# Stick-breaking heads: value products moved behind the next head's scores, result copies ahead of the sigmoids

## The chip, the cores and the metric

The program runs on one core of one Trainium2 chip. The metric is the device time of one launch in microseconds (us). Its engines are TensorE (PE in the profile; its weight loads are a row of their own, PEld), VectorE (DVE), ScalarE (ACT), GpSimd (POOL) and the queue that issues the weight transfers (SP). They run their own instruction streams in order and meet at semaphores.

## The reference

A small language model of two blocks on 512 tokens of width 1024, in fp32. The second block has four layers; layers 0 and 3 mix tokens by "stick-breaking" attention with 8 heads of width 128. Cut to that mixer:

```
for i in range(seq // 128):
    end = (i + 1) * 128
    z = einsum('bhqd,bhkd->bhqk', q[i-th 128 rows], k[:end])
    mask = key < query
    u = where(mask, softplus(z), 0.0)
    a = where(mask, exp(z - rev_cumsum(u)), 0.0)
    out_i = einsum('bhqk,bhkd->bhqd', a, v[:end])
```

The kernel computes the same weights as sigmoid(z) times a running product of sigmoid(-z) from the right. Each of these layers goes on with a memory attention of 4 small heads, an output projection and a gated feed-forward net. Layer 1 has differential attention, layer 2 a short convolution.

## The kernel before, in words

Large matrix products run in three passes on fp32 data split into a high and a low part (high x high, low x high, high x low; function `three`, lines 2625 to 2627, and lines 3369 to 3371 and 3383 to 3385). ACT copies a weight unit to its high part `whi` (line 869), DVE subtracts that from the raw unit and leaves the low part `wlo` (line 1563).

In a stick-breaking layer the input projection is cut in units `n` of 256 output columns, and each unit in four quarters. One quarter is 12 products of 512 columns (or 24 of 256) on PE. Before each quarter stands a slot: slot number `s = 4 * n + q`. Work on the heads is hung into the slots by tables written by hand. For head `h` (0 to 7):

- slot `KQK[h]`: ACT copies q and k of the head to `qk_hi`, DVE makes `qk_lo`.
- slot `KZ[h]`: PE makes the scores z in PSUM (lines 3299 and 2625 to 2627, called "scores" here). ACT takes two sigmoids of them in the same slot (`rest`, then `stick`). One slot later DVE does what I call the chain: a maximum with `upper` in two pieces (line 2379), four scans that form the running product (line 2383), two maskings (line 2388) and the product `stick * rest` (line 2390).
- slot `KTURN[h]`: PE transposes `stick`, 10 blocks of 128x128 (line 3283, "turn"), after the chain has ended. ACT copies the result to `sticks_t` and `sticks_hi`, DVE makes `sticks_lo` (line 2395).
- slot `KPV[h]`: PE multiplies the turned weights with the values (lines 2625 to 2627 on `sticks_hi`, `sticks_lo`, `v_hi`, `v_lo`, then line 3275 in plain fp32; "value product") into PSUM bank 3. It waits for `sticks_lo`, for `v_lo` of its pair of heads, and from the second head on until the result before it has left bank 3. `v_hi` and `v_lo` are made once for two heads, by the even one, two slots ahead of its value product: `at_slot(KPV, s, -2)`. DVE's subtraction for `v_lo` is line 2399, and stands last in its slot.
- the result: ACT copies bank 3 to the high part of `act2`, one slot after the value product (line 1438); DVE subtracts for the low part (`mix_low`, line 2315), two slots after.

Within one slot PE does the value product first, then the turn, then the scores, then the quarter. Slots of the next and the last head interleave: scores of head 1 are in slot 24, between the turn of head 0 (23) and the turn of head 1 (27). In a slot that begins a unit DVE also evicts the last half unit (line 2546, or 2543 for values) and makes `wlo`; it evicts the first half of a unit two slots later.

Of the kernel before, what the change touches and what calls it, by code (L numbers as in the profile page):

```python
# [26 lines left out]
ACT = mybir.ActivationFunctionType  # L27
# [15 lines left out]
NH2, DH2 = 8, 128  # L43
# [29 lines left out]
def wq(i):  # L73
    return P * (i + 1)
# [27 lines left out]
KZ = [20, 24, 28, 32, 36, 40, 47, 52]  # L102
KTURN = [23, 27, 31, 35, 39, 43, 51, 55]
KQK = [18, 22, 26, 30, 34, 38, 46, 50]
KPV = [25, 29, 33, 37, 41, 45, 53, 56]

DZ = [20, 28, 36, 48]

# [2 lines left out]
def at_slot(table, s, after=0):  # L111

    return [h for h, n in enumerate(table) if n is not None and n + after == s]
# [29 lines left out]
def build(nc, A, out, ext_dram):  # L143
    with ExitStack() as ctx:
        sems = {}

        def S(name):
            if name not in sems:
                sems[name] = ctx.enter_context(nc.semaphore(name))
            return sems[name]  # L150
# [3 lines left out]
        def at(name, offset, shape, dt=F32):  # L154
            return nc.alloc_sbuf_tensor_at(name, shape, dt, offset=offset)
# [12 lines left out]
        act2 = at("act2", A0, [P, KF, 2, T], F32R)  # L168
# [114 lines left out]
        def bank(b, w=BANK, off=0):  # L283
            return ps[:, b * BANK + off:b * BANK + off + w]
# [91 lines left out]
        mix_hi, mix_ready = S("mix_hi"), S("mix_ready")  # L376
# [21 lines left out]
        def g_in(l):  # L398
            return G_L0 + sum(evictions(m) + 25 for m in range(l))
# [4 lines left out]
        def evicted(n, half):  # L404

            return n + 1 if n < 2 else 2 + 2 * (n - 2) + half + 1
# [9 lines left out]
        def unit_of(p, stream):  # L416

            return 1 + 3 * p + stream if p >= 2 else (1 + 4 * p + stream if stream < 2 else 3)

        def values_taken(p, last):  # L420

            return evicted(unit_of(p, 2) + (p < 2 and last), 1 if p < 2 else last)
# [90 lines left out]
        def bc(ap2, n):  # L513

            m = ap2.shape[1]
            return ap2.rearrange("p (a m) -> p a m", a=1).broadcast_to([P, n, m])
# [342 lines left out]
        def _(act):  # L859
            a = nc.scalar  # L860
# [556 lines left out]
            def stick_slot(idx, s):  # L1417
                for h in at_slot(KQK, s):
                    n, l = NH2 * idx + h, 3 * idx
                    act.wait_ge(acc_free, g_in(l) + evicted(unit_of(h // 2, 1), h % 2))  # L1420
                    if n:
                        act.wait_ge(S("k_z"), n)
                    for m, b in enumerate((qp, kp)):
                        a.activation(qk_hi[:, m, :], b[h // 2 % 2][:, h % 2, :], ACT.Copy).then_inc(S("qk_hi"), 1)
                for h in at_slot(KPV, s, -2):
                    if h % 2 == 0:
                        n = NH2 * idx + h
                        act.wait_ge(acc_free, g_in(3 * idx) + values_taken(h // 2, 0))
                        if n:
                            act.wait_ge(S("k_o"), n)  # L1430
                        a.activation(v_hi[:, :, :], vp[h // 2 % 2][:, 0:2, :], ACT.Copy).then_inc(S("v_hi"), 1)
                for h in at_slot(KZ, s):
                    act.wait_ge(S("k_z"), NH2 * idx + h + 1)
                    a.activation(rest[:, 0:ZW], ps[:, 0:ZW], ACT.Sigmoid, scale=-1.0).then_inc(S("k_sigmoid"), 1)
                    a.activation(stick[:, :], ps[:, 0:ZW], ACT.Sigmoid).then_inc(S("k_sigmoid"), 1)
                for h in at_slot(KPV, s, 1):
                    act.wait_ge(S("k_o"), NH2 * idx + h + 1)
                    a.activation(act2[:, h, 0, :], bank(3), ACT.Copy).then_inc(mix_hi, 1)
                for h in at_slot(KTURN, s):
                    n = NH2 * idx + h  # L1440
                    act.wait_ge(S("k_tr"), n + 1)
                    if n:
                        act.wait_ge(S("k_o"), n)
                    a.activation(sticks_t[:, :], ps[:, WIDE:ZW], ACT.Copy).then_inc(S("k_at"), 1)
                    a.activation(sticks_hi[:, :], ps[:, 0:WIDE], ACT.Copy).then_inc(S("k_at"), 1)
# [35 lines left out]
            def slot_step(l, s):  # L1481
                memory_slot(l, s)
                if l == 1:
                    differential_slot(s)
                else:
                    stick_slot(l // 3, s)
# [56 lines left out]
        def _(dve):  # L1543
# [3 lines left out]
            def link(ins):  # L1547

                chain[0] += 1
                ins.then_inc(S("vec_chain"), 1)  # L1550
                dve.wait_ge(S("vec_chain"), chain[0])
# [761 lines left out]
            def mix_low(slot, src, n):  # L2313
                dve.wait_ge(mix_hi, n + 1)
                v.tensor_tensor(act2[:, slot, 1, :], src, act2[:, slot, 0, :].bitcast(F32), ALU.subtract).then_inc(mix_ready, 1)
# [50 lines left out]
            def stick_slot(idx, m0, s):  # L2366
                if s == KZ[0]:
                    link(v.memset(rest[:, ZW:ZW + 8], 1.0))
                for h in at_slot(KQK, s):
                    for m, b in enumerate((qp, kp)):  # L2370
                        dve.wait_ge(S("qk_hi"), 2 * (NH2 * idx + h) + m + 1)
                        v.tensor_tensor(qk_lo[:, m, :], b[h // 2 % 2][:, h % 2, :], qk_hi[:, m, :].bitcast(F32),
                                        ALU.subtract).then_inc(S("qk_lo"), 1)
                for h in at_slot(KZ, s, 1):
                    n = NH2 * idx + h
                    dve.wait_ge(S("k_sigmoid"), 2 * n + 1)
                    for b0, step in ((ZQ[0], 384), (ZQ[3] + 384, 256)):
                        d = bass.AP(tensor=rest[:, :].tensor, offset=b0, ap=[[ZW + 8, P], [step, 2], [1, P]])
                        v.tensor_tensor(d, d, bc(upper[:, :], 2), ALU.max).then_inc(S("k_step"), 1)
                    dve.wait_ge(S("k_step"), 9 * n + 2)  # L2380
                    for i in range(4):
                        r = rest[:, ZQ[i]:ZQ[i] + wq(i)][:, ::-1]
                        v.tensor_tensor_scan(out=r, data0=r, data1=ones[:, 0:1].broadcast_to([P, wq(i)]), initial=1.0,
                                             op0=ALU.mult, op1=ALU.mult).then_inc(S("k_step"), 1)
                    dve.wait_ge(S("k_sigmoid"), 2 * n + 2)
                    for b0, step in ((ZQ[0], 384), (ZQ[3] + 384, 256)):
                        d = bass.AP(tensor=stick[:, :].tensor, offset=b0, ap=[[ZW, P], [step, 2], [1, P]])
                        v.tensor_tensor(d, d, bc(mask[:, :], 2), ALU.mult).then_inc(S("k_step"), 1)
                    dve.wait_ge(S("k_step"), 9 * n + 8)
                    v.tensor_tensor(stick[:, :], stick[:, :], rest[:, 1:ZW + 1], ALU.mult).then_inc(S("k_step"), 1)  # L2390
                for h in at_slot(KPV, s, 2):
                    mix_low(h, bank(3), m0 + 2 + h)
                for h in at_slot(KTURN, s):
                    dve.wait_ge(S("k_at"), 2 * (NH2 * idx + h) + 2)
                    v.tensor_tensor(sticks_lo[:, :], ps[:, 0:WIDE], sticks_hi[:, :].bitcast(F32), ALU.subtract).then_inc(S("k_al"), 1)
                for h in at_slot(KPV, s, -2):
                    if h % 2 == 0:
                        dve.wait_ge(S("v_hi"), NH2 * idx + h // 2 + 1)
                        v.tensor_tensor(v_lo[:, :, :], vp[h // 2 % 2][:, 0:2, :], v_hi[:, :, :].bitcast(F32), ALU.subtract).then_inc(S("v_lo"), 1)
# [73 lines left out]
            def attention_slot(l, s):  # L2473
                if l == 1:
                    differential_slot(8 + 10 * l, s)
                else:
                    stick_slot(l // 3, 8 + 10 * l, s)
# [30 lines left out]
            for l in range(NL):  # L2508
# [3 lines left out]
                m0 = 8 + 10 * l  # L2512
# [107 lines left out]
        def _(pe):  # L2620
# [640 lines left out]
            def stick_slot(l, s):  # L3261
                base, m0 = NH2 * (l // 3), 8 + 10 * l
                for h in at_slot(KPV, s):
                    pe.wait_ge(S("k_at"), 2 * (base + h + 1))
# [225 lines left out]
```

## Time and profile before

| | |
|---|---|
| median of 3 runs | 2963.1 us (2962.44 to 2963.11) |
| the profiled execution: its own time | 2963.98 us |
| its span | 2962.3 us |
| PE busy | 2948.2 us (100% of the span) |
| PE weight loads busy | 2652.0 us (90%) |
| DVE busy | 2260.7 us (76%) |
| ACT busy | 1469.7 us (50%) |
| mean granted TensorE clock | 0.999 of full speed |

Busy times are sums over the profiled execution; the engines overlap. The own time is 1.7 us longer than the span, for what lies before the first and behind the last instruction. The two stick-breaking stages lie at about 689 to 835 us and 2427 to 2573 us of the span.

### The profile page before, as it was taken

The numbers are of one execution on the slowest core, as the hardware profiler recorded it, in microseconds if no ns is written. First come the engines' busy times: TensorE is split into PE (matmuls) and PEld (weight loads), VectorE is DVE, ScalarE is ACT, GpSimd is POOL, SyncE is SP. The second block draws the span as 40 slices with busy tenths as digits, with TensorE's granted clock in tenths as the row PEclk, the third lists the DMA queues.
The fourth block names the chain that finished last, engine by engine and source line by source line (L and its number), as shares of the span: only waits on it lengthen the run. The fifth ranks groups of instructions, "written<-read, shape, count | busy, mean of one in ns | idle before, by whom it ended". The sixth has DMA issues, their size and how long they took to land.

```text
span 2962.3 us, 47955 instructions
## 1 busy us (share of the span) xinstructions
PE 2948.2 (100%) x18733; PEld 2652.0 (90%) x18733; DVE 2260.7 (76%) x2788; ACT 1469.7 (50%) x2168; POOL 60.9 (2%) x148
## 2 busy tenths in 40 slices
PE   9999999999999999999999999999999999999999
PEld 8779999888889999878899998888999888889998
DVE  7979888567659887577598875658988568589884
ACT  4576555455345555444455543325555344355553
POOL 6100000000000000000000000000000000000000
PEclk9999999999999999999999999999999999999999
DMA  6232333341133333311333233223333222133332
GB/s 204 60 96 86 113 113 105 109 138 62 56 102 100 99 107 100 105 57 54 106 100 99 96 111 99 82 75 113 107 99 107 93 86 66 56 114 106 99 107 86
DMA packets 261720, 286.98 MB, mean 97 GB/s; under 512 B 12547, under 2 KB 233921, under 8 KB 261577
## 3 DMA queue, kind: packets, MB, share of 16 engines
q1 hardware_dynamic: 261320, 284.69, 30.1%
q8 instruction: 102, 1.67, 0.2%
q14 instruction: 42, 0.34, 0.0%
q10 hardware_dynamic: 256, 0.28, 0.0%
HBM read 280.73 MB, written 5.78 MB: 97 GB/s over the span
## 4 chain that ended last, share of the span: by engine, by line
PE 95%; DVE 3%; ACT 1%; issue 0%; DMA 0%; POOL 0%; ACTq 0%; POOLq 0%; SPq 0%; DVEq 0%
PE ps L2973 40%; PE ps L2625 14%; PE ps L2627 14%; PE ps L2626 14%; PE ps L3383 1%; PE ps L3385 1%; PE ps L3384 1%; PE ps L3283 1%; PE ps L3350 1%; PE ps L3369 1%; PE ps L3370 1%; PE ps L3371 1%; PE ps L3229 1%; PE ps L2876 0%; PE ps L3218 0%
## 5 line engine op out<-in xcount | busy, mean ns | idle before, releaser
L869 ACT ACTIVATE whi<-raw 128x2048 fp32r<-128x2048 f32 (+2 forms) x144 | 246.6, 1712 | 478.7 <-PE ps L2627 371.5
L1563 DVE TENSOR_TENSOR wlo<-raw,whi 128x2048 fp32r<-128x2048 f32 (+2 forms) x144 | 293.6, 2039 | 220.0 <-ACT whi L869 219.7
L2973 PE MATMUL ps<-th,wh 128*128 128x256 f32 x1600 | 453.7, 284 | 0.6 <-DVE wl L1648 0.5
L2973 PE MATMUL ps<-tl,wh 128*128 128x256 f32 x1600 | 452.7, 283 | 0.0
L2973 PE MATMUL ps<-th,wl 128*128 128x256 f32 x1600 | 452.7, 283 | 0.0
L2625 PE MATMUL ps<-hh,whi 128*128 128x512 f32 x896 | 356.1, 397 | 0.0
L2627 PE MATMUL ps<-hh,wlo 128*128 128x512 f32 x896 | 349.5, 390 | 0.0
L2626 PE MATMUL ps<-hl,whi 128*128 128x512 f32 x896 | 349.2, 390 | 0.0
L2973 PE MATMUL ps<-hh,wh 128*128 128x256 f32 x1200 | 340.0, 283 | 0.2 <-DVE gs L1699 0.2
L2973 PE MATMUL ps<-hh,wl 128*128 128x256 f32 x1200 | 339.6, 283 | 0.0
L2973 PE MATMUL ps<-hl,wh 128*128 128x256 f32 x1200 | 339.6, 283 | 0.0
L2973 PEld LDWEIGHTS ps<-th,wh 128*128 128x128 f32 x1600 | 307.0, 192 | 2.3 <-DVE wl L1648 1.1
L2973 PEld LDWEIGHTS ps<-tl,wh 128*128 128x128 f32 x1600 | 307.1, 192 | 0.2
L2973 PEld LDWEIGHTS ps<-th,wl 128*128 128x128 f32 x1600 | 307.1, 192 | 0.0
L2973 PEld LDWEIGHTS ps<-hh,wh 128*128 128x128 f32 x1200 | 230.3, 192 | 0.9 <-DVE gs L1699 0.6
L2973 PEld LDWEIGHTS ps<-hl,wh 128*128 128x128 f32 x1200 | 230.4, 192 | 0.2
L2973 PEld LDWEIGHTS ps<-hh,wl 128*128 128x128 f32 x1200 | 230.3, 192 | 0.0
L2627 PEld LDWEIGHTS ps<-hh,wlo 128*128 128x128 f32 x896 | 168.2, 188 | 35.8
L2625 PEld LDWEIGHTS ps<-hh,whi 128*128 128x128 f32 x896 | 168.3, 188 | 35.6 <-issue 1.7
L2626 PEld LDWEIGHTS ps<-hl,whi 128*128 128x128 f32 x896 | 168.4, 188 | 34.2 <-issue 1.0
L2625 PE MATMUL ps<-acth,whi 128*128 128x512 f32 x504 | 196.5, 390 | 0.0
L2626 PE MATMUL ps<-actl,whi 128*128 128x512 f32 x504 | 196.3, 389 | 0.0
(527 smaller groups left out, 6786.4 us busy)
## 6 DMA issues: line engine op xcount, KB each, us to landing
raw<-in_w_ffn_in SPq DMA_DIRECT2D x88, 1024.0 KB, 5.1
raw<-in_w_in SPq DMA_DIRECT2D x59, 1024.0 KB, 5.3
raw<-in_w_ffn_out SPq DMA_DIRECT2D x40, 1024.0 KB, 5.0
raw<-in_w_o SPq DMA_DIRECT2D x32, 640.0 KB, 4.4
raw<-in_w_gate SPq DMA_DIRECT2D x11, 1024.0 KB, 5.3
raw<-in_w_up SPq DMA_DIRECT2D x11, 1024.0 KB, 5.3
raw<-in_w_down SPq DMA_DIRECT2D x10, 1024.0 KB, 5.1
raw<-in_w_out SPq DMA_DIRECT2D x4, 1024.0 KB, 5.1
```

The costliest lines, as they stand in the source:

```text
L869: a.activation(whi[:, slot, 0:n], raw[:, slot, 0:n], ACT.Copy).then_inc(hi_made, 1)
L1563: v.tensor_tensor(wlo[:, u % 2, 0:n], raw[:, u % 2, 0:n], whi[:, u % 2, 0:n].bitcast(F32), ALU.subtract).then_inc(lo_made, 1)
L2625: mm(dst, wh, xh, start=first, stop=False, skip_group_check=True)
L2626: mm(dst, wh, xl, start=False, stop=False, skip_group_check=True)
L2627: return mm(dst, wl, xh, start=False, stop=last, skip_group_check=True)
L2973: e = mm(bank(b, HALF), wgt[:, q, w], xx, start=start and k == 0 and m == 0, stop=k == KD // 2 - 1 and m == 2, skip_group_check=True)
L3229: e = mm(ps[64 * r:64 * r + 64, o:o + 256], vm[:, l, j, MD * h:MD * h + MD], turned_place(l, m)[:, j, 256 * r:256 * r + 256], start=j == 0 ...
L3283: e = tr(ps[:, o:o + P], stick[:, ZQ[i] + P * j:ZQ[i] + P * j + P], ident[:, :])
L3350: e = mm(ps[:, ZQ[i]:ZQ[i] + wq(i)], qp[hd % 2][:, c, P * i:P * i + P], kp[hd % 2][:, c, 0:wq(i)], start=i != 2, stop=True, skip_group_che ...
L3369: mm(dst, hs, whi[:, slot, w], start=k == 0, stop=False, skip_group_check=True)
L3370: mm(dst, ls, whi[:, slot, w], start=False, stop=False, skip_group_check=True)
L3371: e = mm(dst, hs, wlo[:, slot, w], start=False, stop=k == KD - 1, skip_group_check=True)
```

## The change

The table of the value products gets later slots for heads 0 to 5, in each of the two layers: heads 0 to 4 two slots later, head 5 six. Each of these six now stands in the slot of the next head's turn, and ahead of it, as the order within a slot has it. Heads 6 and 7 keep their slots. What hangs on `KPV` moves along: the result's copy on ACT and its subtraction on DVE, and `v_hi` and `v_lo` of the pair, which stay two slots ahead of the even head's value product. Within a slot ACT now copies the result ahead of the sigmoids, and DVE's `mix_low` comes one slot after the value product in place of two, ahead of the chain.

```
-KPV = [25, 29, 33, 37, 41, 45, 53, 56]
+KPV = [27, 31, 35, 39, 43, 51, 53, 56]
...
+                for h in at_slot(KPV, s, 1):
+                    act.wait_ge(S("k_o"), NH2 * idx + h + 1)
+                    a.activation(act2[:, h, 0, :], bank(3), ACT.Copy).then_inc(mix_hi, 1)
                 for h in at_slot(KZ, s):
                     act.wait_ge(S("k_z"), NH2 * idx + h + 1)
                     a.activation(rest[:, 0:ZW], ps[:, 0:ZW], ACT.Sigmoid, scale=-1.0).then_inc(S("k_sigmoid"), 1)
                     a.activation(stick[:, :], ps[:, 0:ZW], ACT.Sigmoid).then_inc(S("k_sigmoid"), 1)
-                for h in at_slot(KPV, s, 1):
-                    act.wait_ge(S("k_o"), NH2 * idx + h + 1)
-                    a.activation(act2[:, h, 0, :], bank(3), ACT.Copy).then_inc(mix_hi, 1)
...
+                for h in at_slot(KPV, s, 1):
+                    mix_low(h, bank(3), m0 + 2 + h)
                 for h in at_slot(KZ, s, 1):
                     n = NH2 * idx + h
...
-                for h in at_slot(KPV, s, 2):
-                    mix_low(h, bank(3), m0 + 2 + h)
                 for h in at_slot(KTURN, s):
```

On PE, in the first stick-breaking layer, head 0's value product stood in front of the quarter of slot 25:

```order
L2627 MATMUL ps<-hh,wlo 128x512
L2625 MATMUL ps<-sticks_hi,v_hi 128x512
...
L3275 MATMUL ps<-sticks_t,v_pairs 128x256
L3275 MATMUL ps<-sticks_t,v_pairs 128x128
L2625 MATMUL ps<-hh,whi 128x512
```

Now it stands in slot 27, and the turn of head 1 is the next thing behind it:

```order
L2627 MATMUL ps<-sticks_hi,v_lo 128x384
L3275 MATMUL ps<-sticks_t,v_pairs 128x256
L3275 MATMUL ps<-sticks_t,v_pairs 128x128
L3283 MATMUL ps<-ident,stick 128x128 x10
L2625 MATMUL ps<-hh,whi 128x512
```

The two quarters of slots 25 and 26 (24 products) that stood between value product and turn are now in front of both.

On DVE the place is the chain of head 1 and what follows, slots 25 to 29. Before, the subtraction for `v_lo` of heads 0 and 1 was long done by then (slot 23), and the result of head 0 (`act_52`) was dealt with ahead of `sticks_lo`:

```order
L2390 TENSOR_TENSOR stick<-stick,rest 128x1280
L2546 SCALAR_TENSOR_TENSOR kp_191<-ps,rs_63 128x512
L2372 TENSOR_TENSOR qk_lo<-qp_189,qk_hi 128x512
L2372 TENSOR_TENSOR qk_lo<-kp_191,qk_hi 128x512
L2315 TENSOR_TENSOR act_52<-ps,act_52 128x512
L2395 TENSOR_TENSOR sticks_lo<-ps,sticks_hi 128x896
L2546 SCALAR_TENSOR_TENSOR kp_191<-ps,rs_63 128x512
L1563 TENSOR_TENSOR wlo<-raw,whi 128x2048
L2379 TENSOR_TENSOR rest<-rest,upper 128x2x128 x2
```

In the changed program, whose line numbers are two higher here up to the chain:

```order
L2392 TENSOR_TENSOR stick<-stick,rest 128x1280
L2399 TENSOR_TENSOR v_lo<-v_pairs,v_hi 128x512
L2546 SCALAR_TENSOR_TENSOR kp_191<-ps,rs_63 128x512
L2372 TENSOR_TENSOR qk_lo<-qp_189,qk_hi 128x512
L2372 TENSOR_TENSOR qk_lo<-kp_191,qk_hi 128x512
L2395 TENSOR_TENSOR sticks_lo<-ps,sticks_hi 128x896
L2546 SCALAR_TENSOR_TENSOR kp_191<-ps,rs_63 128x512
L1563 TENSOR_TENSOR wlo<-raw,whi 128x2048
L2315 TENSOR_TENSOR act_52<-ps,act_52 128x512
L2381 TENSOR_TENSOR rest<-rest,upper 128x2x128 x2
```

The subtraction for `v_lo` now comes right behind the last product of head 1's chain, and the result's subtraction right ahead of the next chain. The same two moves come again for the pairs of heads 2 and 3 and of heads 4 and 5.

On ACT, slot 28, the result's copy comes between the weight copy and the first sigmoid of head 2:

```order
L869 ACTIVATE whi<-raw 128x2048
L1434 ACTIVATE act_52<-ps 128x512
L1437 ACTIVATE rest<-ps 128x1280
L1438 ACTIVATE stick<-ps 128x1280
L1431 ACTIVATE v_hi<-v_pairs 128x512
```

(the last of these rows in slot 33, behind head 3's sigmoids). Before, the first sigmoid came right behind the weight copy.

## Rows read from the trace of the kernel before

**Rows 1.** The page, parts 1 and 4: busy time, and the chain by engine

```profile
PE 2948.2 (100%) x18733; PEld 2652.0 (90%) x18733; DVE 2260.7 (76%) x2788; ACT 1469.7 (50%) x2168; POOL 60.9 (2%) x148
...
PE 95%; DVE 3%; ACT 1%; issue 0%; DMA 0%; POOL 0%; ACTq 0%; POOLq 0%; SPq 0%; DVEq 0%
```

**Rows 2.** Waits of PE's weight loads: us in total, times, longest

```profile
PEld ps L3283 <- DVE stick L2390: 2.5, 4, 0.9
```

**Rows 3.** Timeline of PE, head 0's value product to head 1's turn

```profile
708.62 0.40 PE L2625 MATMUL ps<-sticks_hi,v_hi 128*128 128x512 f32 x1
...
709.84 0.81 PE L3275 MATMUL ps<-sticks_t,v_pairs 128*128 128x256 f32 x4
710.41 0.48 PE L2625 MATMUL ps<-hh,whi 128*128 128x512 f32 x1
710.73 0.39 PE L2626 MATMUL ps<-hl,whi 128*128 128x512 f32 x1
710.96 0.40 PE L2627 MATMUL ps<-hh,wlo 128*128 128x512 f32 x1
...
715.97 1.25 PE L3283 MATMUL ps<-ident,stick 128*128 128x128 f32 x10
```

**Rows 4.** Timeline of DVE, same stretch: start, duration, instruction, idle before

```profile
703.71 0.68 DVE L2399 TENSOR_TENSOR v_lo<-v_pairs,v_hi 128x512 fp32r<-128x512 f32 x1
...
714.17 0.68 DVE L2546 SCALAR_TENSOR_TENSOR kp<-ps,rs 128x512 f32<-128x512 f32 x1
...
716.77 0.68 DVE L2315 TENSOR_TENSOR act<-ps,act 128x512 fp32r<-128x512 f32 x1
```

**Rows 5.** Timeline of PE, head 2's value product and head 3's turn

```profile
740.38 0.40 PE L2625 MATMUL ps<-sticks_hi,v_hi 128*128 128x512 f32 x1
...
747.72 1.25 PE L3283 MATMUL ps<-ident,stick 128*128 128x128 f32 x10
```

**Rows 6.** Timeline of DVE, head 3's chain

```profile
737.92 2.29 DVE L1563 TENSOR_TENSOR wlo<-raw,whi 128x2048 fp32r<-128x2048 f32 x1 [1.16 <-ACT whi L869]
740.13 0.75 DVE L2379 TENSOR_TENSOR rest<-rest,upper 128x256 f32<-128x256 f32 x2
...
744.58 1.49 DVE L2390 TENSOR_TENSOR stick<-stick,rest 128x1280 f32<-128x1280 f32 x1
745.99 0.68 DVE L2546 SCALAR_TENSOR_TENSOR kp<-ps,rs 128x512 f32<-128x512 f32 x1
```

**Rows 7.** Timeline of ACT, head 3's sigmoids

```profile
737.85 1.24 ACT L1434 ACTIVATE rest<-ps 128x1280 f32<-128x1280 f32 x1
...
746.71 0.63 ACT L1424 ACTIVATE qk_hi<-qp 128x512 fp32r<-128x512 f32 x1 [6.49 <-DVE kp L2546]
```

**Rows 8.** Timeline of PE, head 4's value product and head 5's turn

```profile
772.54 0.40 PE L2625 MATMUL ps<-sticks_hi,v_hi 128*128 128x512 f32 x1
...
779.88 1.25 PE L3283 MATMUL ps<-ident,stick 128*128 128x128 f32 x10
```

**Rows 9.** Timeline of DVE, end of head 5's chain

```profile
778.24 0.68 DVE L2546 SCALAR_TENSOR_TENSOR qp<-ps,rs 128x512 f32<-128x512 f32 x1
```

**Rows 10.** Timeline of PE and DVE at head 6's turn (slot 51)

```profile
807.12 0.28 PE L3370 MATMUL ps<-whi,hl 128*128 128x256 f32 x1
807.24 0.28 PE L3371 MATMUL ps<-wlo,hh 128*128 128x256 f32 x1
807.69 1.31 PE L3283 MATMUL ps<-ident,stick 128*128 128x128 f32 x10 [0.18 <-DVE stick L2390]
808.76 0.36 PE L3369 MATMUL ps<-whi,hh 128*128 128x256 f32 x1
...
806.15 1.49 DVE L2390 TENSOR_TENSOR stick<-stick,rest 128x1280 f32<-128x1280 f32 x1
```

**Rows 11.** Timeline, head 2: end of its chain on DVE, its turn on PE

```profile
728.70 1.49 DVE L2390 TENSOR_TENSOR stick<-stick,rest 128x1280 f32<-128x1280 f32 x1
...
731.85 1.25 PE L3283 MATMUL ps<-ident,stick 128*128 128x128 f32 x10
```

## Prediction, made before the changed kernel was run

> **What bounds the kernel now.** I read the page first: PE is busy in 2948.2 of 2962.3 us, and the chain that ended last runs over PE for 95% of the span [rows 1]. So PE does next to nothing but issue products, the whole program holds 14.1 us in which it is not busy, and a change of order can win only where PE waits for somebody. It can lose wherever it makes PE wait. Next, the waits of the weight loads. In the stages of this change they name one releaser, the end of DVE's chain in front of a turn: 4 waits in both layers together, 2.5 us [rows 2]. Two in each layer: before the turn of head 0, whose place relative to its scores the change leaves alone, and before that of head 6, in slot 51. The latter shows in [rows 10]: DVE's chain ends at 806.15 + 1.49 = 807.64, and PE's first transposition starts at 807.69, so a semaphore costs about 0.05 us. No value product appears among the waits.
>
> Then I put PE's timeline beside DVE's. From one head's value product to the next head's turn PE does the product (708.62 to 710.41, 1.79 us) and two quarters (to 715.97, 5.56 us) [rows 3]. DVE meanwhile works through the next head's chain, without a gap once the weight unit's low part is made [rows 6].
>
> **The change on PE.** The products are the same in number and kind. The value product goes behind the two quarters that followed it. As the turn stays behind all three, it is wanted at the same moment as before for heads 1 to 5, but the value product is now wanted 5.45 us later than it started: 24 products at 0.227 us (0.23 from 710.73 to 710.96 [rows 3]). For the three even heads that is at 708.62 + 5.45 = 714.07 (head 0), 740.38 + 5.45 = 745.83 (head 2) and 772.54 + 5.45 = 777.99 (head 4) [rows 3, 5, 8].
>
> Small gain at the seam: value product ends in plain fp32 (line 3275) and the turn is plain fp32 too. Today the first product of the quarter behind takes 710.73 - 710.41 = 0.32 us in place of 0.23 [rows 3]; one such restart of two goes. The last fp32 product in front of it overlaps it, which is lost. Between 0 and 0.09 us a head; I take 0.03, hence 0.18 for six.
>
> **The change on DVE: v_lo.** This is the term that decides. `v_lo` of a pair was made behind `sticks_lo`, at 703.71 for head 0, and was done 4.2 us before PE wanted it [rows 3, 4]. It now stands two slots ahead of the later value product, in the slot in which DVE runs the next head's chain, and behind this chain. There it takes the place of the eviction (`kp` or `qp`) that follows `stick` today. PE's value product of an even head waits for it, and everything else on PE stands behind that wait, the turn first.
>
> - Head 0. The chain in front is unchanged (no result yet, so no subtraction ahead of it). `v_lo` runs from 714.17 for 0.68 us [rows 4], to 714.85. With 0.05 for the semaphore and 0.1 for a weight load that cannot be made ahead (between 0.03 and the 0.19 of a whole load; I take the half) PE's first product counts from 715.00. Wanted at 714.07: PE waits 0.93 us.
> - Heads 2 and 4. Here the subtraction of the result also comes ahead of the chain, behind `wlo`: 0.68 us (716.77), of which 0.60 counts, since an instruction on DVE starts 0.08 us before the end of the last (744.58 + 1.49 = 746.07, next start 745.99) [rows 4, 6]. `v_lo` would run from 745.99 + 0.60 = 746.59 to 747.27; plus 0.15 is 747.42; wanted at 745.83: 1.59 us. Head 4: 778.24 + 0.60 + 0.68 + 0.15 = 779.67 against 777.99: 1.68 us [rows 6, 8, 9].
> - Head 6 keeps slot 53, and its `v_lo` keeps its place: nothing.
>
> Sum of the new waits: 4.20 us a layer. Layer 3 repeats the pattern and its spacing. A wait does not help the next one, because the chain starts from the scores, which PE issues after the wait. Odd heads find their `v_lo` ready.
>
> **The subtraction ahead of the chain, for the turns.** It delays them only if the chain ends after they are wanted. Head 2's chain ends at 728.70 + 1.49 = 730.19, its turn starts at 731.85 [rows 11]: 1.66 us of room, 1.06 left. Heads with an even head ahead of them (1, 3, 5) have a turn that waits behind the value product anyway. So nothing. The old place of the subtraction was ahead of `sticks_lo`, where DVE waited for ACT; nothing is won by leaving it.
>
> **ACT.** The copy now delays the first sigmoid by some 0.6 us. For head 3 that sigmoid would end at about 739.09 + 0.6 = 739.7 [rows 7], while DVE is busy with `wlo` (to 740.21) and then with the subtraction (to 740.8) [rows 4, 6]. So the copy hides behind DVE's own work; without that cover it would cost another 0.6 in heads 2 and 4. `v_hi` follows the second sigmoid, which now ends near 740.8, and is done before 741.5, long before DVE turns to `v_lo` at 746.6; ACT idles 6.49 us there [rows 7].
>
> **Head 5 and the turn of head 6.** Head 5's value product moves from slot 45 to slot 51, between head 6's scores and head 6's turn. The turn is then wanted 1.79 us later against its chain, and its wait goes. That wait is 807.69 - 807.24 = 0.45 us where 0.12 is usual (807.12 to 807.24), so 0.33, and the ten transpositions behind it take 1.31 us where those of an unheld turn take 1.25: 0.39 us a layer won [rows 3, 10]. What head 6's scores wait for hangs on the quarter of slot 45 and stays.
>
> **Sum.** Per layer 4.20 - 0.39 - 0.18 = 3.63 us lost, for two layers 7.3 us. From the profiled execution's own time, 2963.98, that gives 2971.3. This execution is 0.9 us above the median of the runs, 2963.1, so I predict 2963.1 + 7.3 = 2970.4 us, 0.25% slower. A difference under about 0.2% (5.9 us; above 2969.0 is slower) cannot be told from no change here.
>
> **A rule weighed against a row.** The rows say that a subtraction of 0.68 us put ahead of the chain shifts it by 0.60 us [rows 6]. The Trainium skill (VectorE: DVE Perf Modes, "The DRAIN you can't avoid") says that after each DVE operation a flush of about its duration less 266 ns passes before the next starts. By that rule, an estimate from this page, the subtraction would shift the chain by 0.68 + 0.41 = 1.09 us, and the sum would be 2.0 us larger. The rows show the next start 0.08 us before the end, so the flush, if there is one, lies within the recorded durations; I go by the rows.
>
> **Rivals.**
>
> 1. The value product does not have to wait (the `v_lo` is in time after all, for instance because PE gets there later than I reckon). For it: PE waits for no value product today. Against: three rows put DVE's eviction, whose place it takes, after the moment PE arrives [rows 4, 6, 9]. Time: only the gains are left, 2 x (0.39 + 0.18) = 1.1 us, 2962.0. It decides from the point where `v_lo` ends before 714.0, so the chain would have to be 0.9 us shorter. 8%.
> 2. The result's subtraction does not delay the chain (it slips into DVE's idle time ahead of `wlo`). Against: it stands behind `wlo` in the order, and DVE issues in order. Waits are then 0.93 + 0.99 + 1.08; less 0.57; times two: 4.9 us, 2968.0. 7%.
> 3. The subtraction shifts the chain by twice its 0.60 us, because the copy's delay of the sigmoid adds to it, or because DVE pauses behind it. For it: the sigmoid does start later. Against: DVE starts `rest` before `wlo` has ended, and the sigmoid is done by then [rows 6, 7]. 2 heads x 2 layers x 0.6 = 2.4 us more, 2972.8; the other turns have 1.06 us of room and stay free. 6%. The skill's rule above is of this kind; by the rows it has hardly a chance, and it is counted in the 6%.
> 4. A further wait behind the new ones (the turn's copies on ACT, the scores of the next head that wait for `sticks_lo`): for it, scores follow `sticks_lo` closely. Against: all of these start from the turn, which moves along. 2974 or more. 3%.
> 5. My forecast: 76%, of its own 2969.0 to 2971.8.
>
> Faster by over 0.2% would need 5.9 us of PE waits to vanish in stages where the waits name 2.5 [rows 2]. 1%. Slower: most of 5, with 3 and 4, 0.80. The rest, 0.19, is no difference that shows. Range 2967.2 to 2973.0: it takes in 5, 2 and 3, and leaves out 1 and 4.
>
> **What would show it.** Right: the weight loads of line 2625 on `sticks_hi` appear among the waits, released by DVE `v_lo`, three times in a layer, near 0.8, 1.4 and 1.5 us; the wait before head 6's turn is gone, that before head 0's stays; the spans between the scores of neighbouring heads grow for heads 1-2, 3-4 and 5-6 alone; DVE's `act` subtraction stands between `wlo` and `rest`, 0.60 us before it. Wrong: if these spans keep 15.9 us, rival 1 holds; if head 2's and head 4's waits equal head 0's, rival 2; if turns of heads 2 and 4 wait for `stick`, my room of 1.06 us was mis-read.

## The result, and the profile after

| | before | changed |
|---|---|---|
| median | 2963.5 us (8 runs, 2962.44 to 2966.24) | 2972.33 us (8 runs, 2970.86 to 2972.97) |
| ratio | | 1.0028, 95% interval 1.0019 to 1.0038 |
| profiled execution, own time | 2963.98 us | 2972.01 us |
| its span | 2962.3 us | 2970.3 us |
| start of head 0's turn to start of head 7's value product, layer 0 | 130.17 us | 134.31 us |
| the same, layer 3 | 130.15 us | 134.31 us |

The change made the kernel 8.8 us slower by the medians, 8.0 us by the two profiled executions. The last two lines are differences of start times in the timelines, for layer 0 830.19 - 700.02 before and 833.87 - 699.56 after. They hold 4.14 + 4.16 = 8.3 us, so the whole loss lies in the two stick-breaking stages. I use this stage length below, because it repeats to a few hundredths of a us where medians move by a whole one (subtract_twice below is the exception). One thing that moves the whole time lies outside the stages: in the profiled execution of the kernel before, the granted clock was at its lower level (1.2 GHz) from 136.8 to 140.2 us, and the products from 135.96 to 140.37 us took 4.41 us, where the same ones in the changed kernel's profile took 2.78.

The waits of PE in the changed kernel (engine, line waited for: us in total, times, longest):

```profile
PE ps L2625 <- issue: 6.9, 6, 1.6
PE ps L2701 <- POOL ident L729: 2.1, 1, 2.1
PE ps L2625 <- DVE v_lo L2399: 1.8, 2, 0.9
...
PE ps L3283 <- DVE stick L2392: 0.9, 2, 0.4
```

`v_lo` is named twice, for head 0 of each layer. The waits of heads 2 and 4 are four of the six under "issue"; the other two stand in the same view of before, with 0.8 us together. Read by the names alone, this view would have hidden three quarters of the loss. The last experiment shows why. The wait of a turn for `stick` has gone from four times to two; [rows 2] has the four as waits of the weight loads.

The timelines show who is waited for. Head 0, PE and DVE:

```profile
713.37 0.39 PE L2627 MATMUL ps<-hh,wlo 128*128 128x512 f32 x1
714.65 0.47 PE L2625 MATMUL ps<-sticks_hi,v_hi 128*128 128x512 f32 x1 [0.90 <-DVE v_lo L2399]
714.97 0.39 PE L2626 MATMUL ps<-sticks_lo,v_hi 128*128 128x512 f32 x1
...
712.31 1.49 DVE L2392 TENSOR_TENSOR stick<-stick,rest 128x1280 f32<-128x1280 f32 x1
713.72 0.68 DVE L2399 TENSOR_TENSOR v_lo<-v_pairs,v_hi 128x512 fp32r<-128x512 f32 x1
```

The bracket counts idle time by the modelled end of the last product. The real hole is between starts: 714.65 - 713.37 = 1.28 us where products stand 0.23 apart, and the first product then takes 714.97 - 714.65 = 0.32. So head 0 costs 1.05 + 0.09 = 1.14 us. DVE made `v_lo` exactly where `kp` was evicted before [rows 4]: right behind `stick`.

Head 2, PE, and the whole of head 3's chain on DVE:

```profile
746.18 0.39 PE L2627 MATMUL ps<-hh,wlo 128*128 128x512 f32 x1
748.07 0.48 PE L2625 MATMUL ps<-sticks_hi,v_hi 128*128 128x512 f32 x1 [1.50 <-issue]
748.39 0.43 PE L2626 MATMUL ps<-sticks_lo,v_hi 128*128 128x512 f32 x1
...
738.52 2.29 DVE L1563 TENSOR_TENSOR wlo<-raw,whi 128x2048 fp32r<-128x2048 f32 x1 [1.32 <-ACT whi L869]
740.73 0.68 DVE L2315 TENSOR_TENSOR act<-ps,act 128x512 fp32r<-128x512 f32 x1
741.33 0.75 DVE L2381 TENSOR_TENSOR rest<-rest,upper 128x256 f32<-128x256 f32 x2
...
745.77 1.49 DVE L2392 TENSOR_TENSOR stick<-stick,rest 128x1280 f32<-128x1280 f32 x1
747.18 0.68 DVE L2399 TENSOR_TENSOR v_lo<-v_pairs,v_hi 128x512 fp32r<-128x512 f32 x1
```

Against [rows 6] the chain starts 741.33 - 738.52 = 2.81 us behind `wlo`'s start where it was 2.21: the subtraction of the result costs it 0.60. The hole on PE is 1.89 - 0.23 = 1.66 us. The restart is slow here too: from its first product to the turn behind it head 2's value product takes 1.98 us, and head 1's, which waits for nothing, 1.87. With these 0.11 head 2 costs 1.77 us. Head 4 has the same picture: products at 780.11 and 782.08, a hole of 1.75 us, and 1.95 us for the value product, together 1.84.

ACT in the same slot: the copy (`act`) does stand in front of the first sigmoid, which ends at 738.86 + 1.23 = 740.09, before DVE wants it at 741.33.

```profile
736.56 1.92 ACT L869 ACTIVATE whi<-raw 128x2048 fp32r<-128x2048 f32 x1 [1.53 <-PE ps L2627]
738.39 0.58 ACT L1434 ACTIVATE act<-ps 128x512 fp32r<-128x512 f32 x1
738.86 1.23 ACT L1437 ACTIVATE rest<-ps 128x1280 f32<-128x1280 f32 x1
```

In slot 51 head 5's value product and head 6's turn run without a hole, where [rows 10] had one of 0.33:

```profile
809.45 0.28 PE L3371 MATMUL ps<-wlo,hh 128*128 128x256 f32 x1
809.57 0.40 PE L2625 MATMUL ps<-sticks_hi,v_hi 128*128 128x512 f32 x1
...
810.79 0.81 PE L3275 MATMUL ps<-sticks_t,v_pairs 128*128 128x256 f32 x4
811.44 1.25 PE L3283 MATMUL ps<-ident,stick 128*128 128x128 f32 x10
```

Sum of a layer: 1.14 + 1.77 + 1.84 = 4.75 of waits, less the forecast gains of 0.39 and 0.18, 4.18; measured 4.14 and 4.16.

### The profile page after: what moved, and what is told of

The parts are those of the page before. It is cut to its first block, busy times and chain, and to the rows that moved or that the text cites. A ratio compares the mean times of both kernels' runs of the same rounds, so it can differ in the third digit from the quotient of the medians.

```text
span 2970.3 us, 47955 instructions
## 1 busy us (share of the span) xinstructions
PE 2947.2 (99%) x18733; PEld 2649.8 (89%) x18733; DVE 2260.1 (76%) x2788; ACT 1468.6 (49%) x2168; POOL 61.9 (2%) x148
## 4 chain that ended last, share of the span: by engine, by line
PE 92%; DVE 4%; ACT 1%; issue 1%; SPq 1%; DMA 1%; ACTq 0%; DVEq 0%
PE ps L2973 39%; PE ps L2625 13%; PE ps L2626 13%; PE ps L2627 13%; PE ps L3369 1%; PE ps L3371 1%; PE ps L3370 1%; PE ps L3383 1%; PE ps L3385 1%; PE ps L3384 1%; PE ps L3283 1%; PE ps L3350 1%; SPq L583 1%; PE ps L3229 1%; PE ps L2876 0%
```

## Experiments

My theory: PE waits in front of the value products of heads 0, 2 and 4 for `v_lo`, which the change put behind a chain; the result's subtraction ahead of the chain makes two of the three waits longer. Rivals: the results' new order costs by itself, or a value product right ahead of a turn does.

**v_early.** `v_hi` and `v_lo` back in their old slots, the value products and results as changed. The second edit stands twice, on ACT and on DVE.

```
+KVAL = [23, None, 31, None, 39, None, 51, None]
-                for h in at_slot(KPV, s, -2):
+                for h in at_slot(KVAL, s):
```

> The changed kernel with v_hi and v_lo of heads 0 to 5 made in their slots of before (23, 31, 39), everything else as changed. Theory 1 (PE waits for v_lo in front of the value products of heads 0, 2 and 4: 1.15, 1.8 and 1.8 us a layer in the changed kernel's trace): all these waits go, only the gains are left, 2 x (0.39 + 0.18) = 1.1 us; about 2962 us where before has 2963.1, ratio 0.9996, and 9.5 us less than changed. Theory 2 (the cost comes from the results' copy and subtraction put ahead of the chain): v_lo is early but the chain still 0.6 us later, so at least a third of the loss stays, 2966 or more. Theory 3 (a value product right ahead of a turn costs by itself, through ACT and DVE): the whole loss stays, 2971.

Measured: 2962.09 us against 2963.52, ratio 0.9995 (0.9986 to 1.0004); the stages take 129.62 and 129.59 us, 0.55 and 0.56 less than before. By the time alone this is no difference to before; it is 10 us less than the changed kernel's median. The waits for `v_lo` are gone, and of PE's waits for DVE in these stages only that of head 0's turn is left:

```profile
PE ps L3284 <- DVE stick L2393: 0.9, 2, 0.4
```

Value product and turn stand back to back:

```profile
713.72 0.39 PE L2628 MATMUL ps<-hh,wlo 128*128 128x512 f32 x1
713.95 0.40 PE L2626 MATMUL ps<-sticks_hi,v_hi 128*128 128x512 f32 x1
...
715.17 0.81 PE L3276 MATMUL ps<-sticks_t,v_pairs 128*128 128x256 f32 x4
715.82 0.27 PE L3284 MATMUL ps<-ident,stick 128*128 128x128 f32 x1
```

The chains of heads 2 to 5 still start 2.81 us behind `wlo`'s start here, as in the changed kernel, and value products still stand ahead of turns, and neither costs anything. Theories 2 and 3 fall. The two gains together are as large as forecast (0.57 a layer). This run moves `v_hi` along with `v_lo`; v_ahead_of_chain below moves `v_lo` alone.

**copies_only.** The table of before, the results' new order alone.

```
-KPV = [27, 31, 35, 39, 43, 51, 53, 56]
+KPV = [25, 29, 33, 37, 41, 45, 53, 56]
```

> The changed kernel with the table of value products of before: only the order of the results' copy and subtraction is changed. In these slots the copy and the sigmoids never share a slot, so the subtraction comes one slot earlier, in the slot behind the chain. Theory 1: no difference to before, ratio 1.0000 within the interval. Theory 2 (the new order of the results costs by itself): slower than before by some us.

Measured: 2963.54 against 2963.52, ratio 1.0000 (0.9990 to 1.0009), stages 130.17 and 130.16 us, as before. The new order does nothing while it does not stand ahead of a chain.

**head5_only.** Only head 5's value product moved.

```
-KPV = [27, 31, 35, 39, 43, 51, 53, 56]
+KPV = [25, 29, 33, 37, 41, 51, 53, 56]
```

> The changed kernel with the value products of heads 0 to 4 back in slots 25, 29, 33, 37, 41; only head 5 stays moved, from slot 45 to 51, and the results keep their new order. Theory 1: no wait for v_lo, the wait ahead of head 6's turn is gone (0.39 us a layer) and one restart: 2 x 0.42 = 0.8 us less than before, ratio 0.9997. Rival (the wait ahead of head 6's turn only moves to the scores of head 7 or to a value product): within 0.2 us of before, and the trace names the new wait.

Measured: 2962.36 against 2963.52, ratio 0.9997 (0.9988 to 1.0006), stages 129.70 and 129.73 us: 0.47 and 0.42 less than before. The one wait goes and none comes for it.

**result_behind_v.** For heads 0 to 4 DVE's subtraction of the result goes from ahead of the chain to behind the chain and `v_lo` (the second piece of the diff).

```
                 for h in at_slot(KPV, s, 1):
-                    mix_low(h, bank(3), m0 + 2 + h)
+                    if h > 4:
+                        mix_low(h, bank(3), m0 + 2 + h)
...
+                for h in at_slot(KPV, s, 2):
+                    if h < 5:
+                        mix_low(h, bank(3), m0 + 2 + h)
```

> The changed kernel with DVE's subtraction for the results of heads 0 to 4 taken from ahead of the chain to behind it and behind v_lo; the value products and v_lo stay as changed. Theory 1 with its second term (the subtraction shifts the chain and v_lo of heads 2 and 4 by 0.60 us): these two waits shrink by 0.6 us each, 4 x 0.6 = 2.4 us less than changed, head 0's wait stays as it is; about 2969. Rival (the subtraction costs the chain nothing): no difference to changed, 2971.4. Rival (it costs twice): 4.8 us less, 2966.6.

Measured: 2975.51, ratio 1.0041 (1.0028 to 1.0055), stages 136.37 us each, 2.06 more than the changed kernel. A miss, and mine: I had seen what the subtraction delays and not who waits for it. The value product of the next head does, since it writes the same bank 3:

```profile
PE ps L2629 <- DVE act L2315: 9.2, 8, 1.7
```

Head 1, which waited for nothing, shows it, PE and DVE:

```profile
730.08 0.39 PE L2631 MATMUL ps<-hh,wlo 128*128 128x512 f32 x1
731.41 0.48 PE L2629 MATMUL ps<-sticks_hi,v_hi 128*128 128x512 f32 x1 [0.94 <-DVE act L2315]
...
729.06 1.49 DVE L2393 TENSOR_TENSOR stick<-stick,rest 128x1280 f32<-128x1280 f32 x1
730.47 0.68 DVE L2315 TENSOR_TENSOR act<-ps,act 128x512 fp32r<-128x512 f32 x1
```

So once the value products are late and share one bank, the subtraction is better ahead of the chain: there it costs two waits 0.60 us each, here it makes heads 1 and 3 wait and takes nothing from heads 2 and 4.

**two_banks.** As result_behind_v, with the value products of heads 1, 3 and 5 in bank 6, so that each waits only for the result two heads back. The result's copy and subtraction read bank 6 for these heads (not shown).

```
-                        pe.wait_ge(mix_ready, m0 + 2 + h)
+                        pe.wait_ge(mix_ready, m0 + 2 + (h if h > 5 else h - 1))
-                        dst, keys, c = bank(3, T - P * j, P * j), ...
+                        dst, keys, c = bank(3 + 3 * (h in (1, 3, 5)), T - P * j, P * j), ...
```

> As result_behind_v (the results' subtraction of heads 0 to 4 behind the chain and behind v_lo), and the value products of heads 1, 3 and 5 go to PSUM bank 6 in place of bank 3, so that a value product no longer has to wait for the result before it. This frees the question that result_behind_v left: what the subtraction ahead of the chain costs the value products of heads 2 and 4. Theory 1 (0.60 us each): the waits of heads 2 and 4 fall from 1.8 to 1.2 us, heads 1 and 3 wait for nothing, 2.4 us less than the changed kernel. Rival (the chain starts no earlier, since something else holds it): same time as the changed kernel. Rival (the wait for the result comes through another semaphore): slower than the changed kernel, as result_behind_v was.

Measured: 2969.58 us, ratio 1.0021 (1.0012 to 1.0030); the changed kernel on the same chip 2971.22. Stages 133.16 and 133.19 us: 2.3 us less than the changed kernel in the two together. The hole of head 2 is 747.48 - 746.19 = 1.29 us between starts, down from 1.89, and `v_lo` follows a chain that starts 0.6 us earlier:

```profile
746.19 0.39 PE L2631 MATMUL ps<-hh,wlo 128*128 128x512 f32 x1
747.48 0.48 PE L2629 MATMUL ps<-sticks_hi,v_hi 128*128 128x512 f32 x1 [0.91 <-issue]
...
745.17 1.49 DVE L2393 TENSOR_TENSOR stick<-stick,rest 128x1280 f32<-128x1280 f32 x1
746.59 0.68 DVE L2400 TENSOR_TENSOR v_lo<-v_pairs,v_hi 128x512 fp32r<-128x512 f32 x1
```

The term of 0.60 us is shown from this side.

**changed_again.** The changed kernel as it is, run beside two_banks and subtract_twice.

> The changed kernel itself, once more on the chip of the two kernels beside it, so that a few us between them can be told: by all theories its ratio to before is again 1.0028, some 8 us more.

Measured: 2971.22 us, ratio 1.0028 (1.0018 to 1.0039), stages 134.36 and 134.33 us.

**subtract_twice.** And from the other side: the subtraction doubled for heads 1 and 3.

```
                 for h in at_slot(KPV, s, 1):
+                    if h in (1, 3):
+                        dve.wait_ge(mix_hi, m0 + 2 + h + 1)
+                        link(v.tensor_tensor(act2[:, h, 1, :], bank(3), act2[:, h, 0, :].bitcast(F32), ALU.subtract))
                     mix_low(h, bank(3), m0 + 2 + h)
```

> The changed kernel with DVE's subtraction for the results of heads 1 and 3 done twice, one behind the other, ahead of the chain. Theory 1: the chain, and v_lo behind it, move 0.65 to 0.7 us further (one more subtraction and a wait for its end), so the waits ahead of the value products of heads 2 and 4 grow from 1.8 to 2.5 us: 4 x 0.7 = 2.8 us more than the changed kernel. Rival (these value products wait for something other than v_lo behind the chain): no difference. The flush of the Trainium skill (VectorE: DVE Perf Modes, The DRAIN you can't avoid) would make it 4 x 1.1 = 4.4 us.

Measured: 2979.46 us (2975.94 to 2980.88), ratio 1.0054 (1.0040 to 1.0068). The wait does what theory 1 says: DVE starts the second subtraction 0.72 us behind the first and the chain 0.61 behind that, and the hole ahead of head 2's value product is 2.61 us between starts where it was 1.87 in changed_again beside it. Four such make 2.9 us. But the median is 8.2 us above changed_again. The timeline of PE shows where more comes from:

```profile
745.22 0.39 PE L2630 MATMUL ps<-hh,wlo 128*128 128x512 f32 x1
747.83 0.47 PE L2628 MATMUL ps<-sticks_hi,v_hi 128*128 128x512 f32 x1 [2.22 <-issue]
748.14 0.39 PE L2629 MATMUL ps<-sticks_lo,v_hi 128*128 128x512 f32 x1
748.36 0.56 PE L2630 MATMUL ps<-sticks_hi,v_lo 128*128 128x512 f32 x1
748.72 0.53 PE L2628 MATMUL ps<-sticks_hi,v_hi 128*128 128x384 f32 x1
749.04 0.53 PE L2629 MATMUL ps<-sticks_lo,v_hi 128*128 128x384 f32 x1
```

A product of 384 columns takes 0.32 us from start to start, where the same product takes 0.18 in v_early and even one of 512 columns only 0.23 [rows 3]. The windows of this stretch say why (the last number but two is the granted clock):

```profile
core 0: us, PE busy (x) PEld busy (x) DVE busy (x) ACT busy (x) POOL busy (x), PEclk, DMA share, GB/s
745.30:747.80 2.50, 0.31 (x2) 0.00 (x1) 2.46 (x4) 0.00 (x0) 0.00 (x0) 1.00 0.00 0
747.80:751.60 3.80, 3.77 (x14) 3.45 (x15) 1.71 (x3) 1.15 (x2) 0.00 (x0) 0.58 0.00 0
751.60:755.00 3.40, 3.40 (x19) 2.95 (x19) 0.98 (x1) 1.30 (x2) 0.00 (x0) 0.96 0.00 0
```

Behind a hole of 2.4 us the granted clock fell from its upper level (2.4 GHz) to its lower (1.2 GHz) for most of the 3.8 us that follow. This profiled execution, whose own time 2975.94 is the lowest of the five, has one such fall, in layer 0: that stage took 137.34 us, the one of layer 3 without a fall 135.77.

**subtract_twice_again.** The same kernel once more.

> subtract_twice once more, since its runs spread over 5 us where those of other kernels spread over 3, and its median lies 8 us above the changed kernel where its waits account for 3.0. If the excess belongs to the kernel: again 2976 to 2981 and again a first stage 1.5 us longer than the waits explain. If it belonged to the runs: 2974.

Measured: 2979.31 us (2973.68 to 2979.69), ratio 1.0048 (1.0034 to 1.0062). It belongs to the kernel, and it is the clock: this profiled execution (span 2977.6) has the fall behind head 4's value product of layer 0 and two more in layer 3; its stages took 137.43 and 139.04 us, where 135.8 is the length without one. So a fall costs about 1.6 us. The changed kernel's 2971.2 with 2.9 of waits and none to four such falls gives 2974 to 2981, an estimate; the ten runs lie between 2973.7 and 2980.9, and only the two profiled ones show their falls one by one. The stretch over head 4's hole of layer 0, and the one behind it:

```profile
779.70:782.30 2.60, 0.34 (x2) 0.00 (x0) 2.57 (x4) 0.00 (x0) 0.00 (x0) 1.00 0.01 3
782.30:787.00 4.70, 4.64 (x21) 4.34 (x21) 0.45 (x1) 0.00 (x0) 0.00 (x0) 0.64 0.00 0
```

In the changed kernel's own profile the granted clock does not fall anywhere in the two stages, behind holes of up to 1.75 us. That is no safe length, though: before, v_early and copies_only show a fall near 137 us, outside the stages, 0.6 to 0.8 us after PE goes on from a wait for DVE (1.58 us between starts, 1.2 us of them idle). All twelve profiles have this wait, and nine have no fall behind it. What decides stays open.

**v_ahead_of_chain.** `v_lo` in the changed slot, but ahead of the chain.

```
+                for h in at_slot(KPV, s, -2):
+                    if h in (0, 2, 4):
+                        dve.wait_ge(S("v_hi"), NH2 * idx + h // 2 + 1)
+                        v.tensor_tensor(v_lo[:, :, :], vp[h // 2 % 2][:, 0:2, :], v_hi[:, :, :].bitcast(F32), ALU.subtract).then_inc(S("v_lo"), 1)
                 for h in at_slot(KZ, s, 1):
...
                 for h in at_slot(KPV, s, -2):
-                    if h % 2 == 0:
+                    if h == 6:
```

> The changed kernel with DVE's v_lo of heads 0, 2 and 4 in the same slot as changed but ahead of the chain in place of behind it. DVE then waits for v_hi, which ACT makes behind the two sigmoids of the neighbouring head. By the rows of the changed kernel the chain would start 1.4 to 1.9 us later than in before, and a turn has 1.66 us of room in before. Theory 1: the value products no longer wait for v_lo; the turns of heads 3 and 5 begin to wait for the chain by up to 0.4 us each, that of head 1 does not. About 2962 to 2964, 8 us less than the changed kernel. Rival (the place of v_lo relative to the chain does not matter, DVE's load does): same time as the changed kernel.

Measured: 2963.36 us against 2962.66, ratio 1.0002 (0.9992 to 1.0011), stages 130.24 us each, 4.1 less than the changed kernel and 0.6 more than v_early. No value product waits for `v_lo`. DVE has the same work in the same slot as in the changed kernel, so it is the place behind the chain that costs, not DVE's load. The room of the turns is used up: head 5's turn starts 0.2 us late, head 3's 0.1 in layer 3, and head 4's scores, behind head 3's turn, 0.3.

**v_wait_last.** PE's waits ahead of a value product in another order.

```
                     pe.wait_ge(S("k_al"), base + l // 3 * NH2 // 2 + h + 1)
-                    pe.wait_ge(S("v_lo"), base + h // 2 + 1)
                     if h:
                         pe.wait_ge(mix_ready, m0 + 2 + h)
                     pe.wait_ge(acc_free, g_in(l) + values_taken(h // 2, 1))
+                    pe.wait_ge(S("v_lo"), base + h // 2 + 1)
```

> The changed kernel with PE's wait for v_lo put last of the five waits ahead of a value product (it is the third; the waits for the result before and for the evictions follow). In the changed kernel PE's first product starts 0.25 us after v_lo has ended, where a turn, which has one wait, starts 0.05 us after its chain. Theory 1 (the waits behind the third one are gone through one by one, each costs some 0.05 to 0.1 us): that distance falls from 0.25 to 0.05 to 0.15 us. Rival (it is the load of the first weights that takes the time): it stays at 0.25 us. The time moves by at most 1.2 us, less than one run can tell.

Measured, one execution of 2971.32 us: the distance from `v_lo`'s end to the first product is 748.00 - 747.86 = 0.14 us at head 2, 0.21 in the changed kernel (748.07 - 747.86). Before rounding the distance is 0.15 us at all six holes, where the changed kernel has 0.21 at heads 2 and 4 and 0.26 at head 0 of both layers. So the satisfied waits behind do cost, 0.07 us where there are two of them (heads 2 and 4) and 0.11 where there is one (head 0); their number does not explain the size. The stages are 134.06 and 134.04 us, 0.3 less than the changed kernel. The greater effect is on the view of waits: all six holes now bear the name of `v_lo`. In the changed kernel heads 2 and 4 had two waits behind that for `v_lo` and stood under "issue"; head 0 had one and kept the name.

```profile
PE ps L2625 <- DVE v_lo L2399: 7.5, 6, 1.5
```

## Why the prediction was right

- **That PE waits for `v_lo` at heads 0, 2 and 4, and nowhere else.** Right. The six holes are there, v_early takes all of them away by moving `v_hi` and `v_lo`, v_ahead_of_chain by moving `v_lo` alone, and the odd heads wait for nothing.
- **Their size, 0.93, 1.59 and 1.68 us.** Too small: measured 1.14, 1.77 and 1.84, 0.55 us more in a layer. The step that fell short is "0.05 for the semaphore and 0.1 for a weight load". Head 0's `v_lo` ends at 714.40 and the product starts at 714.65, 0.26 later before rounding, and the value product then takes 0.08 longer: 0.33 us in place of 0.15 (0.33 and 0.30 at heads 2 and 4). Two things were left out: the satisfied waits behind the late one (0.11 and 0.07, by v_wait_last), and the slow first product, which I had in hand for the seam [rows 3] and did not count here. With the late wait last, the start alone comes 0.15 us behind `v_lo`, just my sum, but that is luck: the weight load starts 0.12 us behind it and the product 0.03 behind the load, not 0.05 and 0.1. The rest, 0.04 in a layer, is `v_lo` itself, a little later against the wanted time than reckoned. Twice 0.55 is 1.1 us, and the stages (8.3) differ from my sum (7.3) by 1.0.
- **The subtraction ahead of the chain costs it 0.60 us.** Right: read directly in the changed kernel, taken away in two_banks (2.3 us less, 2.4 forecast), added in subtract_twice. The second one of subtract_twice shifted the chain by 0.73 us more (it waits for the end of the first). Rival 2 falls by it, and so does rival 3: the chain starts 0.60 us behind the start of the subtraction, not 1.2. By the flush of the Trainium skill (VectorE: DVE Perf Modes, "The DRAIN you can't avoid") it would have been 1.09, an estimate, and 4.4 us in subtract_twice, where 2.9 were measured. The trace does not agree with that rule as I applied it; the same section says that a next operation that is not held starts earlier, which I had left out.
- **The copy hides behind DVE's work; the turns keep their room.** Right; no turn but head 0's waits. Head 2's turn starts 1.02 us behind its chain's end (1.06 forecast). In v_ahead_of_chain the chains of heads 3 and 5 start 1.66 us later against `wlo` than before, and that is more than head 5's turn had room for.
- **Head 6's turn and the seam, 0.57 us a layer.** Right: 0.55 in v_early, 0.42 to 0.47 for head 5 alone (0.42 forecast), which leaves 0.1 for the other five seams (0.15 forecast).
- **The total.** 2970.4 forecast, 2972.33 measured. Of these 1.9 us, 0.4 is before's median, 2963.1 from 3 runs then and 2963.5 from 8 now. Of the other 1.5 (7.3 us more forecast, 8.8 measured) some 1.0 is the size of the waits, and the rest is within the spread of the medians: changed_again lay 8.1 us above before beside it. So the time fell above the 2969.0 to 2971.8 that I gave my own forecast, and nearer to rival 3's 2972.8. The time alone could not have told the two apart; the 0.60 us in the trace does.
- **What I said would show it.** Two of the signs failed, the others held. The waits did not appear under the name of `v_lo` for heads 2 and 4. And the spans between scores grew for heads 1-2 (15.89 to 16.98) and 3-4 (15.87 to 17.61), but not for 5-6 (26.15 to 26.02). Head 4's wait lies in that span, but I forgot that head 5's value product, 1.79 us, leaves it for the next one, 6-7, which grew from 17.60 to 19.06. In v_early, without the wait, span 5-6 is 24.26.

Of the rival times, 2962.0 (no wait for `v_lo`) is that of v_early, 2962.09: the price of the rival was right, only its condition did not hold.

No version beats the kernel of before by more than can be told from run times. In their stages v_early (ratio 0.9995) and head5_only (0.9997) are shorter by 1.1 and 0.9 us in two layers.

## What to carry to other kernels

When an operation is moved in a table, look for everything else keyed to the same entry: here what it needs (`v_lo`) moved with it, to behind a long chain of another engine, and cost eight times what the move gave. Before an engine that is always busy a late helper costs its full lateness, so place producers by when the chain on their own engine lets them run, not by a fixed distance from the consumer. And judge a wait by the holes between starts: a view that names the last of several semaphores can put the same hole under another name.

## What the runs showed of the hardware

- A hole of 2.4 to 2.5 us on PE can bring the granted clock down to its lower level, with about 1.6 us lost each time on top of the hole; it happened behind 1 of 4 such holes in one profiled execution (subtract_twice) and 3 of 4 in another (subtract_twice_again). In the two stages it was not seen behind holes of up to 1.8 us, but elsewhere in the program it was, behind a wait of 1.58 us between starts, in 3 of 12 profiles.
- A product right behind a wait starts 0.15 us after its late input if its wait is the last in order (v_wait_last), 0.21 us with two satisfied waits behind it and 0.26 us with one (changed kernel, heads 2 and 4, and head 0). The value product that it begins then takes 0.08 to 0.11 us longer than unheld.
